# Hybrid SSD, band attention and MoE step: bias products of an expert pass moved from ahead of the first gate/up chunk to behind the third

## The reference, cut to what matters

```
MoE, top 4 of 32, D_MODEL = D_FF = 1024, tokens grouped by expert:
gu   = xb @ w_gate_up[e] + b_gate_up[e]
gate = min(gu[:, :D_FF], 7);  up = clip(gu[:, D_FF:], -7, 7)
act  = (up + 1) * gate * sigmoid(1.702 * gate)
y    = act @ w_down[e] + b_down[e]
out  = sum over a token's 4 experts of gate weight * y
```

## Time and profile before

| | |
|---|---|
| median of three runs | 1292.07 us (1290.39 to 1294.35) |
| the profiled execution | 1290.63 us |
| its span, first to last instruction | 1288.7 us |
| TensorE (PE) busy | 1252.5 us, 97% |
| VectorE (DVE) busy | 490.8 us, 38% |
| ScalarE (ACT) busy | 207.9 us, 16% |
| HBM read | 432.33 MB |

### The profile page before, as it was taken

How to read it: one execution, slowest core, us unless ns; L and a number is a source line. 1 busy time by engine, 2 the same in 40 slices (tenths; PEclk the granted TensorE clock), 3 DMA queues, 4 the chain that set the end, 5 groups by cost and what they waited for, 6 DMA issues and landing times.

```text
span 1288.7 us, 17301 instructions
## 1 busy us (share of the span) xinstructions
PE 1252.5 (97%) x6444; PEld 549.3 (43%) x6445; DVE 490.8 (38%) x987; ACT 207.9 (16%) x407; POOL 36.9 (3%) x62
## 2 busy tenths in 40 slices
PE   7999999999999999999999999999999999999996
PEld 5755654664333343333333333333334333334332
DVE  2633444457533343333332333323334233233334
ACT  1131134452210010101101001110001010011102
POOL 2000003400000000000000000000000000000000
PEclk9999999999999999999999999999999999999998
DMA  9623126037999969999997999997999999699995
GB/s 321 219 77 121 66 82 214 25 132 292 421 426 427 428 276 426 427 430 426 429 419 290 427 428 427 427 427 307 398 427 428 427 428 426 284 428 428 426 426 201
DMA packets 48010, 436.33 MB, mean 339 GB/s; under 512 B 6229, under 2 KB 7373, under 8 KB 19318
## 3 DMA queue, kind: packets, MB, share of 16 engines
q1 hardware_dynamic: 43984, 429.41, 80.2%
q0 software_dynamic: 2080, 6.48, 1.5%
q10 hardware_dynamic: 1926, 0.18, 0.1%
HBM read 432.33 MB, written 3.72 MB: 338 GB/s over the span
## 4 chain that ended last, share of the span: by engine, by line
PE 85%; DMA 11%; DVE 2%; issue 1%; ACT 0%; POOL 0%; SPq 0%; DVEq 0%; POOLq 0%
PE PS L1822 34%; PE PS L1862 16%; DMA ring<-in_w_gate_up_dram 11%; PE PS L1320 7%; PE PS L1329 5%; PE PS L1275 5%; PE PS L1780 5%; PE PS L1748 4%; PE PS L1331 1%; PE PS L1617 1%; PE PS L1805 1%; PE PS L1591 1%; PE PS L1472 1%; PE PS L1458 1%; PE PS L1475 0%
## 5 line engine op out<-in xcount | busy, mean ns | idle before, releaser
L1822 PE MATMUL PS<-ring,r 128*64 128x512 f32 x2304 | 519.9, 596 | 11.5 <-DMA ring<-in_w_gate_up_dram 11.0
L1822 PEld LDWEIGHTS PS<-ring,r 128*64 128x64 f32 x2304 | 158.8, 137 | 314.1 <-issue 281.3
L1862 PE MATMUL PS<-ring,r 128*64 128x512 f32 x1152 | 255.1, 595 | 0.2
L1145 DVE SCALAR_TENSOR_TENSOR r<-PS,gprev,r 128x512 f32<-128x512 f32 (+1 forms) x222 | 152.5, 742 | 113.5 <-PE PS L1780 112.0
L1862 PEld LDWEIGHTS PS<-ring,r 128*64 128x64 f32 x1152 | 82.2, 137 | 148.2 <-issue 146.1
L1247 DVE TENSOR_TENSOR yy<-PS,yy 128x512 fp32r<-128x512 f32 x36 | 24.9, 692 | 249.6 <-ACT yy L736 249.6
L727 ACT ACTIVATE r<-r 128x512 f32<-128x512 f32 x36 | 22.7, 629 | 504.2 <-DVE r L1230 504.2
L1230 DVE TENSOR_SCALAR r<-PS 128x512 f32<-128x512 f32 x36 | 24.9, 692 | 202.3 <-PE PS L1822 202.3
L1275 PE MATMUL PS<-ident,r 128*128 128x128 f32 (+5 forms) x490 | 81.9, 298 | 10.1 <-DVE r L771 9.2
L1320 PE MATMUL PS<-r,ring 128*128 128x323 f32 x320 | 90.1, 438 | 0.0
L1275 PEld LDWEIGHTS PS<-ident,r 128*128 128x128 f32 (+5 forms) x490 | 62.7, 186 | 36.1 <-issue 18.2
(11 more groups left out here) (317 smaller groups left out, 749.6 us busy)
## 6 DMA issues: line engine op xcount, KB each, us to landing
ring<-in_w_gate_up_dram SPq DMA_DIRECT2D x96, 2048.0 KB, 16.3
ring<-in_w_down_dram SPq DMA_DIRECT2D x64, 2048.0 KB, 16.6
ring<-in_w_gate_up_dram SPq DMA_DIRECT2D x64, 1024.0 KB, 16.3
ring<-in_w_in_dram SPq DMA_DIRECT2D x8, 2048.0 KB, 13.9
ring<-in_w_out_dram SPq DMA_DIRECT2D x3, 2048.0 KB, 7.6
r<-in_x_prompt_dram SPq DMA_DIRECT2D x2, 512.0 KB, 3.7
r<-in_x_prompt_dram POOLq DMA_DIRECT2D x2, 512.0 KB, 4.5
r<-bias_table_clipped SPq DMA_DIRECT2D x4, 256.0 KB, 7.0
```

The lines of the kernel that those rows point to most:

```text
L1145: v.scalar_tensor_tensor(xx, PS[0:rows, out_banks(t)[h], :], gprev[0:rows, t:t + 1], xx, ALU.mult, ALU.add)\
L1822: last = mm(PS[64 * h:64 * h + 64, m, :], xt[:, k % 4, k // 4, :], w[:, kk, D * m + 512 * h:D * m + 512 * h + 512], start=False, stop=(k = ...
L1862: last = mm(PS[64 * h:64 * h + 64, 2, :], at[:, kk, c, :], w[:, kk, 512 * h:512 * h + 512], start=(c == 0 and kk == 0), stop=(c == 1 and k ...
```

## The change

The four bias matmuls of a pass no longer come first. They stand behind chunk 2, and gs_used2, which frees the slot of chunk 2, now comes from the last of them. The first matmul of chunk 0 starts the sums (start=True). VectorE makes sel for the next pass when gs_used2 has come, where it waited for gs_used before.

```
@@ VectorE, expert_pass
-                dve.wait_ge(s["gs_used"], b + 1)
+                dve.wait_ge(s["gs_used2"], b + 1)
                 selector(e_next)
                 dve.wait_ge(s["gate_mm"], b + 1)
@@ TensorE, expert_pass
                 pe.wait_ge(s["xt_ev"], b + 1)
-                pe.wait_ge(s["sel_ready"], b + 1)
-                for m in range(2):
-                    for h in range(2):
-                        mm(PS[64 * h:64 * h + 64, m, :], sel[:, :], b_gu3[:, D * m + 512 * h:D * m + 512 * h + 512],
-                           start=True, stop=False)
                 for c in range(GU_CHUNKS):
...
-                                      start=False, stop=(k == KD - 1))
+                                      start=(k == 0), stop=(k == KD - 1))
+                        return last
+
+                    def biases():
+                        pe.wait_ge(s["sel_ready"], b + 1)
+                        for m in range(2):
+                            for h in range(2):
+                                last = mm(PS[64 * h:64 * h + 64, m, :], sel[:, :],
+                                          b_gu3[:, D * m + 512 * h:D * m + 512 * h + 512], start=False, stop=False)
                         return last
...
+                        if c == GU_CHUNKS - 2:
+                            last = biases()
                         last.then_inc(s[("gs_used", "gs_used1", "gs_used2")[c]], 1)
```

## The result

The changed kernel is slower: 1295.51 us in the median (1291.9 to 1300.78, 18 runs) against 1292.24 us (1290.0 to 1295.57, 18 runs) for the kernel before. The ratio is 1.0026, with a 95% interval of 1.0017 to 1.0035. The forecast was 1290.7, in a range of 1288.3 to 1293.6; the time lies above the range.

What follows compares the result with a forecast made beforehand. TensorE was taken to bound most passes and a DMA-TensorE loop three stretches; 3 x 0.43 = 1.3 us plus 0.09 ahead of the first restart gave 1.4 us less, median 1292.07 to 1290.7, range 1288.3 to 1293.6.

Steps and rivals of the forecast that it cites:

- the loop from restart to restart: Chunk 0 freed, DMA moves seven experts unbroken, TensorE finishes and frees chunk 0 again; three such stretches, 217.0 to 217.4 us.
- the bias at 0.43 us at either place: Four bias matmuls on TensorE: 0.43 us ahead of chunk 0 or behind chunk 2, so sum 0 in non-waiting passes.
- VectorE's wait at nothing: VectorE makes sel later, after the bias matmuls; TensorE needs it only behind chunk 2 of the next pass: cost 0.
- a pass of 26.51 us: A TensorE pass that waits for no weights takes 26.51 us and still does after the change.
- The bias between chunks 2 and 3 of a waiting pass: Twenty matmuls need 4.37 of 4.95 us, leaving 0.58; the bias needs 0.43 and fits with 0.15 over.
- Rival (c): Bias breaks the gate/up run at a fixed 0.20 us each time: 4.4 us more, 1296.5; 4 in 100.
- rival (d): Combine comes 0.43 us earlier and meets a low part from VectorE that is not ready: slower; 1 in 100.
- (b): More stretches are DMA's, so up to five starts gain 0.43 us each: 2.2 us, 1289.9; 6 in 100.
- (e): Bias leaves the path in all passes, through a gap behind chunk 2: 12.5 us, 1278; 2 in 100.
- Rival (a): Bias exposed in waiting passes, or DMA starves at the first down chunk; each loop loses its 0.43: 1292.1; 10 in 100.
- the sentence on the distances behind a restart: First down chunk, issued 19.2 then 19.6 us after the restart, while DMA is busy until 19.6: loss taken as 0.
- the three gains of 0.43 us: Earlier release of chunk 0 shortens TensorE's part of each of three loops by 0.43 us: 1.3 us less.

Runs made afterwards that it cites:

- e7: Changed kernel with the bias matmuls behind chunk 0, whose release comes from the last of them, VectorE waiting for gs_used: 1291.69 us, 0.9997 of before.
- e11: Kernel before with only VectorE's selector wait moved to gs_used2: 1291.28 us, 1.0001 of before.
- e14: Repeat of the changed kernel with the first eight combine matmuls moved behind chunk 1: 1288.97 us, 0.9971 of before.
- e13: Changed kernel with chunk 1 loaded as two halves, the first released earlier, combine where it was: 1291.38 us, 0.9983 of before.
- e5: Kernel before with the first eight combine matmuls of a loop pass behind chunk 1 instead of chunk 0: 1290.74 us, 0.9987 of before.
- e4: Changed kernel with the first down chunk loaded as two halves, the first issued some 1.7 us earlier: 1292.17 us, 1.0006 of before.
- e8: Kernel before with the first down chunk loaded as two halves: 1293.01 us, 1.0009 of before.
- e6: Changed kernel with the two gate bias matmuls first in the pass again, only the two up ones behind chunk 2: 1294.27 us, 1.0018 of before.
- e3: Changed kernel with chunk 2 released ahead of the bias and VectorE waiting for a semaphore from the last bias matmul: 1295.05 us, 1.0029 of before.
- e1: Kernel before with the first down chunk released later, by the first matmul of the second down chunk: 1298.21 us, 1.0052 of before.
- e9: Changed kernel with the first eight combine matmuls behind chunk 1: 1289.53 us, 0.9983 of before.
- e12: Kernel before with the first down chunk released 0.84 us late and the first eight combine matmuls behind chunk 1: 1292.50 us, 1.0006 of before.
- e2: Changed kernel with chunk 0 released later in loop passes, by the second combine matmul: 1291.54 us, 0.9998 of before.

## Why the prediction was wrong

**Right:** the loop from restart to restart, three of them, as what sets the time; the bias at 0.43 us at either place, with nothing on top that shows (e7); VectorE's wait at nothing (e11, to within about 1.5 us); a pass of 26.51 us; 0.42 us less in the tail of the loop that was looked at. The bias between chunks 2 and 3 of a waiting pass is hidden too: chunk 2 starts at 664.28, the bias at 667.76, and the last half of chunk 3 at 669.25, 4.97 us behind chunk 2, where it was 4.95. Rival (c) and rival (d) didn't happen, nor (b) or (e). Rival (a) named the right place, DMA short at the first down chunk, but with the wrong price.

**The step that failed** is the sentence on the distances behind a restart: "the last one just in time. It has a little more [...] I take 0 for it; at worst the 0.43 is lost again." Two things are wrong in it. The first is the margin. I set the moment of issue against the moment when DMA has nothing left. But a transfer that meets an idle DMA has its last landing 7.1 to 7.6 us after its issue, behind all four restarts of every trace, and it needs 4.90 when DMA is at work. By that difference it must be issued an estimated 2.2 to 2.7 us ahead. I had seen that DMA isn't at full rate in the first 2 us behind a restart, and drew nothing from it for the margin. The Trainium skill, DMA: Bandwidth & Descriptors, section Anatomy of one DMA — SWDGE (gpsimd) path, states a fixed cost of about 2.0 us beside the bytes, fitted to transfers that GpSimd issues, and by this fit a transfer of 2.1 MB would take an estimated 6.8 us. These are issued by SyncE, and the traces have 0.3 to 0.8 us more.

The second is the bound. I took it that DMA can't lose more than the 0.43 by which it is early. At the down chunk it loses 0.6 to 2.0 us each time, because a few of the 16 engines fall back by up to 2.1 us, and TensorE waits for all. So the three gains of 0.43 us became losses of 1.8, 1.2 and 1.2 us, of which 0.7 to 0.8 in the first two loops fell at chunk 1. With the shortage cured in either of two ways (e14, e13), the kernel is 0.3% and 0.2% faster than before, but this is the cure and the change together: combine's move alone (e5) is worth 0.13%. What the change is worth by itself is seen only in the restarts, 0.5 us in two loops of e4 against e8 and 0.1 to 0.2 of e14 against e5.

Two readings were off without effect on the sum. The full rate holds from the eleventh slice on, not from the tenth (292 GB/s). And the three loops are 15.1 us longer than their passes, of which the 15 waits of the earlier trace rows cover 11.0; the rest isn't accounted for in the prediction.

**What stays open** is why a short lead at the down chunk mostly costs 0.6 to 2.1 us after a short lead at chunk 1, and 0 to 0.8 us without one. T4 is a rule read from one profiled execution of each kernel. With a short lead at both chunks (e6, changed, e3, e1) 13 of 16 down chunks have an extra over 0.5; with a long one at chunk 1 (e14, e9, e13, e12) it is 2 of 16, both in e12, whose slower runs have no trace. What in the DMA engines makes it so isn't shown. It isn't the size of chunk 1's own extra: where that is largest (1.34 in the changed kernel, 1.76 in e3, 1.50 in e1) the one at the down chunk is the smallest of its kernel. Nor does the latency of an idle DMA explain the loss: behind a restart the first packet moves 0.97 us after the issue, and here engines that ran out 1.7 us after an issue stood still for over a microsecond more. Also, of before, e2, e5, e7 and e11, with leads of 2.36 to 2.61, two restarts of 20 had a dear extra (e7, e11): before stands near the edge itself. That may be a part of its own scatter of 6 to 8 us; this isn't shown.

## What to carry to other kernels

A load that follows a release is late some time before the queue is empty: here, with a short lead at chunk 1 too, the loss came at each restart whose lead at the down chunk was 2.15 us or less, at some with 2.2 to 2.4, and at none with more. With a long lead at chunk 1 little came of it. A change that frees one buffer earlier moves all the others later against it. So compute the lead of each transfer in the burst behind a restart, not only of the one that moves, and look at all 16 landings: one late engine is a late transfer. And when DMA catches up with TensorE after a pause, smooth the releases (here eight matmuls moved behind the second chunk) before you advance the first.

## What the hardware did that I had not expected

A DMA engine that gets its next work a few tenths later doesn't lose a few tenths. In the changed kernel two to five of 16 engines landed 1.2 to 2.1 us behind the others and stayed there for the 190 us to the end of the stretch. For some four microseconds at the start of this the rate stood at 336 to 352 GB/s, while the DMA share was 0.95 to 1.02. The share thus doesn't show this loss; the rate, the number of packets under way and the spread of the 16 landings do (0.6 to 1.1 us before, 2.1 to 2.7 after, from the first down chunk behind the first three restarts on). And it is neither certain nor proportional: with a lead of 2.23 to 2.38 us it came at two of four restarts, at its full size.
